# Two fused transformer blocks on one core: the modulation, the state-space quarters and the key selection are put in another order on five engines

## The chip, the cores and the metric

The kernel runs on one core of a Trainium2 chip. The time is device microseconds for one execution. The core has TensorE (matmuls and transposes, named PE in the profile; its weight loads are PEld), VectorE (DVE), ScalarE (ACT), GpSimd (POOL) and SyncE (SP), which here only issues DMAs. Each engine runs its own list of instructions in order; semaphores tie the lists together. All arithmetic is float32.

## The reference

Two blocks in series on x of 512 rows by 1024. Only block one is touched by the change.

```
mod = silu(c) @ w_ada + b_ada                  # shift, scale, gate: 3 x 1024
h = rms_norm(x, norm_g) * (1 + scale) + shift
u, z, q, k, v, az, q_idx, k_idx, w_idx = split(h @ w_in)   # 512 each; k_idx 64, w_idx 8
y = s5(u) + d_skip * u                         # 32 groups of 16 channels, 64 complex states
y = gelu(y); y_ssm = y * sigmoid(y @ w_glu + b_glu) * silu(z)
score = sum over heads of w_idx * relu(q_idx . k_idx), causal; sel = top 128 keys of each query
y_attn = softmax(q . k / 8 + rel_bias, over sel) @ v * silu(az)   # 8 heads of 64, q and k normed
x = x + gate * (concat(y_ssm, y_attn) @ w_out)
x = second_block(x)                            # sparse attention, pooling mixer, conv feed-forward
```

## The kernel before

Everything lives in one SBUF arena; two slots of 2 MB take turns for the weights (chunks `u`, `qi`, `ki`, `k`, `v`, `q`, `az`, `z`, `gate0`, `gate1`, `glu`, `out0`, `out1`, ...), loaded by SyncE, a chunk two places on waiting for the last matmul on the one that it replaces. PSUM banks 0 to 3 take the projections (`name_proj`), banks 4 to 7 the transposes and the small products (`name_aux`); TensorE must take the names in the order in which they were given. `proj_ready`/`aux_ready` wait for TensorE to have filled a bank, `proj_out`/`aux_out` for it to have been emptied. `step` puts a semaphore wait between two instructions of one engine that depend on each other. The order within each engine is written out by hand.

**Start.** x arrives as four row tiles. ScalarE squares and sums each (L1233). VectorE turns the sums into means (`x_mean`), GpSimd raises them to -0.5 (L1593), and VectorE (tiles 0 and 2, L1869) and ScalarE (tiles 1 and 3, L1236) scale x. TensorE turns x (eight banks, `x_turns`), ScalarE copies it out to hT. The modulation is w_ada times silu(c), in four parts of 2 MB: VectorE's `mod_sums(s)` is eight 128x512 multiply-adds (L1851, L1854) into `macc[s % 2]`, TensorE's `mod_turn(s)` adds over the partitions (L773), VectorE's `mod_cols(s)` and `h_odd` and ScalarE's `h_even` apply the result to hT. Parts 0 and 1 serve the first half of the channels, so that `u_step(0)` can begin; parts 2 and 3 serve `u_step(1)`. Between the two u steps TensorE turns the state-space matrices b and c (L732, L788) and the relative bias (L794). VectorE then makes the tables of powers; its `prep_done` lets GpSimd begin.

**The state-space product** goes by quarters q of eight groups. GpSimd makes `CL` (three 128x1152 operations, L1624 to L1626) and `Zt` (three 128x1024, L1634 to L1636), then `r8` and `E1`, `E2` (seven of about 512, L1641 to L1652). TensorE's `ssm_kernels(q)` makes the taps from CL and turns Zt; `ssm_chunks(q)` gives the chunk inputs; GpSimd rotates them (L1660 to L1663), VectorE scans (`scan(q)`, L1994), GpSimd rotates back (L1665 to L1668, `s_done`), with two swaps of halves through DMAs of SyncE (`ssm_swap`). `ssm_out(q)` on TensorE needs `s_done` and the spread taps (`ssm_spread`), and reads CL as well; `ssm_back(q)` takes y out over DRAM to where VectorE's `gelu_in(q)` reads it. There is one CL, so that GpSimd begins quarter q + 1 when TensorE has finished `ssm_out(q)`.

**Attention of block one.** `rels(i, ...)` are the index heads of query block i (1 to 3; eight heads), taken by ScalarE with relu into two buffers `reluq` and summed by VectorE (`scores(i)`, L2001 to L2010). `topk(i, rounds)` takes eight keys a round (maximum, L2016; replacement, L2017) over 256, 384 or 512 columns, 16 rounds each. `head_norm` squares, sums, takes the root of (eleven small steps, L1774 to L1779) and scales (L2033) q or k; TensorE turns k (`kt`) and q (`qt`) after it. Then 16 pairs of heads are worked off: scores, two filler matmuls (L967, L969: the gate and the GLU), turned weights, values. The first filler waits for `silb_done`, which VectorE gives after its work on the mixer. The rounds of block 3 lie in part between the first three pairs, and `gelu_in(3)`, `gelu_out(3)` at pairs 1 and 3. After the pairs comes the output projection, and from there on block two.

## Time and profile before

| | us |
|---|---|
| median of three runs | 1527.62 |
| the three runs | 1523.86, 1527.62, 2513.14 |
| the profiled execution | 1530.01 |
| its span, first to last instruction | 1528.2 |
| TensorE busy in it | 1441.4 (94%) |
| VectorE, ScalarE, GpSimd busy | 631.3, 317.1, 262.8 |
| mean granted clock of TensorE | 0.970 |

The profiled execution is one run; the times of single instructions below come from it. A busy TensorE counts waiting out a slow clock as busy: a matmul takes twice as long at 1.2 GHz (granted clock 0.50) as at 2.4 GHz (1.00).

### The profile page before, as it was taken

How to read it: one execution, taken by the hardware profiler on the slowest of the kernel's cores; microseconds unless marked ns; L12 is line 12 of the kernel's file. 1: busy time of each engine (PE TensorE's matmuls, PEld its weight loads, DVE VectorE, ACT ScalarE, POOL GpSimd, SP SyncE). 2: the span in 40 equal slices, each digit the busy share in tenths (PEclk: the TensorE clock that was granted, in tenths of full speed). 3: DMA queues.
4: the chain of work that ended last, by engine and by line, in shares of the span. 5: the costliest groups of instructions: out<-in, count | busy, mean ns of one | idle time of the engine just before them, and what ended most of it. 6: DMA issues, size and time to landing. Idle time of an engine off the chain costs nothing.

```text
span 1528.2 us, 13916 instructions
## 1 busy us (share of the span) xinstructions
PE 1441.4 (94%) x5076; PEld 723.4 (47%) x5076; DVE 631.3 (41%) x1533; ACT 317.1 (21%) x773; POOL 262.8 (17%) x257
## 2 busy tenths in 40 slices
PE   2799999969999998998999999998999999989999
PEld 2444455534545446454555565444444444434343
DVE  6571759888431660033456673112323333230000
ACT  3111232114200002202456662001111111110000
POOL 1053627624102478000000000000000000000000
PEclk9799999979999998999999999999999999999999
DMA  9345233442312222102110001203113132121220
GB/s 325 119 104 157 69 84 96 137 132 76 138 33 68 77 89 74 64 1 83 56 50 7 1 2 56 101 9 110 55 57 108 55 102 63 42 110 38 89 87 27
DMA packets 85630, 120.43 MB, mean 79 GB/s; under 512 B 15128, under 2 KB 43102, under 8 KB 85564
## 3 DMA queue, kind: packets, MB, share of 16 engines
q1 hardware_dynamic: 79088, 109.89, 22.4%
q10 hardware_dynamic: 4732, 5.97, 1.2%
q0 software_dynamic: 1744, 3.70, 0.8%
q8 instruction: 41, 0.67, 0.2%
q14 instruction: 25, 0.20, 0.0%
HBM read 111.00 MB, written 6.84 MB: 77 GB/s over the span
## 4 chain that ended last, share of the span: by engine, by line
PE 86%; DVE 8%; ACT 2%; issue 2%; DMA 1%; POOL 0%; SPq 0%; ACTq 0%; DVEq 0%
PE bank L1198 20%; PE bank L704 19%; PE bank L1208 10%; PE bank L714 6%; PE bank L1157 5%; PE bank L732 4%; PE bank L999 4%; PE bank L1113 3%; PE bank L1137 3%; PE bank L763 2%; PE bank L1011 2%; PE bank L872 1%; DVE arena L1854 1%; PE bank L1095 1%; DVE arena L2017 1%
## 5 line engine op out<-in xcount | busy, mean ns | idle before, releaser
L704 PE MATMUL bank<-arena 128*128 128x512 f32 (+1 forms) x752 | 319.0, 584 | 3.4 <-ACT arena L1459 3.0
L1198 PE MATMUL bank<-arena 128*128 128x512 f32 (+1 forms) x704 | 302.5, 592 | 1.5 <-ACT arena L1453 1.5
L704 PEld LDWEIGHTS bank<-arena 128*128 128x128 f32 x752 | 143.0, 192 | 167.6 <-issue 162.5
L1198 PEld LDWEIGHTS bank<-arena 128*128 128x128 f32 (+1 forms) x704 | 131.9, 188 | 171.5 <-issue 171.5
L1208 PE MATMUL bank<-arena 128*128 128x512 f32 (+1 forms) x352 | 156.0, 602 | 5.0 <-DVE arena L2401 4.0
L732 PE MATMUL bank<-arena 128*128 128x128 f32 (+2 forms) x692 | 98.5, 283 | 35.3 <-ACT arena L1236 10.6
L732 PEld LDWEIGHTS bank<-arena 128*128 128x128 f32 (+2 forms) x692 | 84.1, 146 | 91.0 <-issue 43.1
L2390 DVE SCALAR_TENSOR_TENSOR arena<-bank,arena 128x511 f32<-128x511 f32 (+1 forms) x44 | 33.0, 749 | 211.9 <-ACT arena L1572 211.9
L714 PE MATMUL bank<-arena 128*128 128x512 f32 x256 | 111.5, 593 | 0.0
L1208 PEld LDWEIGHTS bank<-arena 128*128 128x128 f32 (+1 forms) x352 | 66.1, 191 | 95.0 <-issue 90.1
L1593 POOL TENSOR_TENSOR arena<-arena 128x1 f32<-128x1 f32 x12 | 8.1, 682 | 509.9 <-DVE arena L1785 496.6
L2373 DVE SCALAR_TENSOR_TENSOR arena<-bank,arena 128x512 f32<-128x512 f32 x16 | 11.1, 692 | 203.0 <-PE bank L1208 152.3
L1572 ACT ACTIVATE arena<-bank,arena 128x512 f32<-128x512 f32 (+1 forms) x44 | 34.2, 777 | 258.6 <-PE bank L1198 258.6
L1534 ACT ACTIVATE arena<-arena 128x128 f32<-128x128 f32 (+3 forms) x128 | 70.9, 555 | 73.2 <-DVE arena L2321 73.2
L1157 PE MATMUL bank<-arena 128*128 128x512 f32 x160 | 85.2, 639 | 0.6 <-DVE arena L2356 0.5
L2321 DVE CUSTOM_DVE_ANT_0 arena<-bank,arena 128x128 f32<-128x128 f32 (+3 forms) x128 | 57.8, 489 | 62.3 <-PE bank L1113 61.5
L714 PEld LDWEIGHTS bank<-arena 128*128 128x128 f32 x256 | 48.1, 190 | 57.9 <-issue 57.9
L999 PE MATMUL bank<-arena 128*128 128x512 f32 x128 | 55.7, 593 | 0.5 <-issue 0.5
L1113 PE MATMUL bank<-arena 64*128 64x128 f32 (+3 forms) x256 | 51.8, 481 | 1.2 <-ACT arena L1524 1.2
L1546 ACT ACTIVATE arena<-bank 128x128 f32<-128x128 f32 (+3 forms) x128 | 47.9, 424 | 19.3 <-PE bank L732 19.3
L1137 PE MATMUL bank<-arena 128*64 128x128 f32 x640 | 48.9, 282 | 0.0
L2335 DVE TENSOR_SCALAR arena<-arena 128x128 f32<-128x128 f32 (+3 forms) x128 | 43.7, 384 | 2.3
(307 smaller groups left out, 1497.7 us busy)
## 6 DMA issues: line engine op xcount, KB each, us to landing
arena<-in_w_in SPq DMA_DIRECT2D x14, 2048.0 KB, 7.8
arena<-in_w_up SPq DMA_DIRECT2D x20, 1024.0 KB, 6.8
arena<-in_w_ada SPq DMA_DIRECT2D x8, 1024.0 KB, 14.4
arena<-in_w_down SPq DMA_DIRECT2D x4, 2048.0 KB, 7.7
arena<-in_w_ada SPq DMA_DIRECT2D x2, 2048.0 KB, 8.3
arena<-in_w_out SPq DMA_DIRECT2D x2, 2048.0 KB, 7.9
arena<-in_w_attn_br SPq DMA_DIRECT2D x2, 2048.0 KB, 8.8
arena<-in_w_o SPq DMA_DIRECT2D x2, 2048.0 KB, 7.7
```

Of the source, the lines that this page charges most:

```text
L704: mm = pe.matmul(ps[:, 0:n], act[:, k, 128 * t:128 * t + 128], w[:, k, 0:n], start=(k == 0), stop=(k == kt - 1))
L714: mm = pe.matmul(ps[:, :], w[:, k, 128 * j:128 * j + 128], act[:, k, :], start=(k == 0), stop=(k == kt - 1))
L732: mm = pe.transpose(ps[0:f, at:at + p], b, ident[0:p, 0:p] if eye is None else eye)
L999: mm = pe.matmul(ps[:, :], a[:, 128 * t:128 * t + 128], w[:, k, :], start=(n == 0), stop=(n == KT - 1))
L1113: pe.matmul(bank[2 * (n % 2) + e][:, 0:128 * (i + 1)], qT2[r, p, 128 * i:128 * i + 128], ksT[r, 2 * b + p // 4, 0:128 * (i + 1)], start=Tr ...
L1137: mm = pe.matmul(ps[64 * e:64 * e + 64, 0:128], vs2[:, b, m, 64 * g:64 * g + 64], pT2[:, n % 2, e, 128 * m:128 * m + 128], start=False, st ...
L1157: mm = pe.matmul(fbank(key)[:, :], act_[:, k, 128 * t:128 * t + 128], w[:, k, :], start=(k == 0), stop=(k == kt - 1))
L1198: mm = pe.matmul(ps[0:m, :], w[:, k, c0:c0 + m], hT[:, k, :], start=(k == 0), stop=(k == KT - 1))
L1208: mm = pe.matmul(banks[t][:, :], aT[0:m, k, 128 * t:128 * t + 128], w[0:m, k - 8 * b, :], start=(k == 0), stop=(k == FT - 1))
L1534: act.activation(buf, buf, ACT.Exp, scale=-1.0, bias=sml[:, c0:c0 + 1], accum_out=sml[:, c1:c1 + 1]).then_inc(exp2_done, 1)
L1546: act.activation(pT2[:, n % 2, e, 0:128 * (i + 1)], abank(("pt2", n, e))[:, 0:128 * (i + 1)], ACT.Copy).then_inc(afree(("pt2", n, e)), 1)
L2321: v.tensor_tensor_reduce(pr2[:, n % 3, e, 0:cols], bank[2 * (n % 2) + e][:, 0:cols], trim[:, 512 - cols:512], -1.0, 3.0e38, ALU.add, ALU.m ...
```

## The change

It does four things, all in block one.

1. At the start GpSimd makes mean and root of each row tile itself and ScalarE scales all four; VectorE does neither. The loads of b and c go from ScalarE's queue to SyncE's, ahead of the load of u's weights and of modulation parts 2 and 3. TensorE turns c, b and the relative bias before `mod_turn(0)`, and VectorE's `mod_cols(2)` comes after the cosine instead of ahead of `mod_sums(3)`.
2. CL gets a second buffer (in qiT, so that quarter 1 waits for the last index head). GpSimd begins quarter q when it has finished the rotations of quarter q - 1 and `ssm_out(q - 2)` is done.
3. The index heads run beside k's projection instead of v's, and `scores` and the selection come earlier on VectorE: all of block 3's rounds lie ahead of `scan(2)`, q's norm and the pairs. The quarters are spread anew over the projections on TensorE, ScalarE and SyncE; the bias load (2 MB, `biasT`) is issued earlier and waits for `r8_done`.
4. `gelu_in` has three operations instead of four, the constant going into tanh's scale, and all four channels' GELU lie ahead of the pairs.

The diff, cut to its core; the bank names (`name_aux`) follow the new order, and `CLs[q % 2]` stands for CL in `ssm_taps` and `ssm_out`:

```diff
@@ -119,6 +119,7 @@
 Wn = z.take(1024, QG, 128)
+CLs = [CL, qiT.rearrange("p a b -> p (a b)")[:, 0:QG * 9 * GC].rearrange("p (a b c) -> p a b c", a=QG, b=9)]
 KX0 = z.at
@@ -576,6 +578,12 @@
     ada_load(1)
+    for a, src in enumerate((b_re, b_im)):
+        for half in range(2):
+            sp_.dma_start(braw[a][0:32, 1024 * half:1024 * half + 1024],
+                          src[0].rearrange("g p i -> g (p i)")).then_inc(b_in, 16)
+    for a, src in enumerate((c_re, c_im, c_re)):
+        sp_.dma_start(craw[:, :, a, :], src[0].rearrange("(m g) o p -> (g o) m p", g=8)).then_inc(craw_in, 16)
     wu_load(0)
@@ -631,18 +639,18 @@
             ssm_swap(0)
+            ssm_back(0)
         if name == "az":
-            ssm_back(0)
             ssm_spread(1)
+            ssm_swap(1)
         if name == "z":
-            ssm_swap(1)
             ssm_back(1)
-        if name == ("gate", 0):
             ssm_spread(2)
             ssm_swap(2)
+        if name == ("gate", 0):
             ssm_back(2)
+            ssm_spread(3)
         if name == ("gate", 1):
-            ssm_spread(3)
             ssm_swap(3)
@@ -793,6 +797,10 @@
                   start=True, stop=True).then_inc(aux_done, 1)
+    pe.wait_ge(pool_ones, 1)
+    mod_turn(0)
+    mod_turn(1)
+    u_step(0)
     mod_turn(2)
@@ -856,18 +864,11 @@
     ssm_kernels(0)
-    one_rows("k", 0, "k", hT)
-    ssm_chunks(0)
-    one_rows("k", 1, "k", hT)
-    one_rows("k", 2, "k", hT)
-    one_rows("k", 3, "k", hT)
-    ssm_out(0)
-    one_rows("v", 0, "v", hT)
...
-        w = weights(pe, "v")
-        ps = begin_proj(("v", t)) if half == 0 else pbank(("v", t))
+        w = weights(pe, "k")
+        ps = begin_proj(("k", t)) if half == 0 else pbank(("k", t))
         for k in range(4 * half, 4 * half + 4):
@@ -886,39 +887,45 @@
     for i in range(1, TT):
-        half_rows(i, 0)
+        half_rows(i - 1, 0)
         rels(i, range(0, 4))
-        if i == 2:
-            ssm_kernels(1)
-        half_rows(i, 1)
+        half_rows(i - 1, 1)
         rels(i, range(4, 8))
+        if i == 1:
+            ssm_chunks(0)
+    ssm_out(0)
+    one_rows("k", 3, "k", hT)
+    one_rows("v", 0, "v", hT)
+    ssm_kernels(1)
+    one_rows("v", 1, "v", hT)
     ssm_chunks(1)
+    one_rows("v", 2, "v", hT)
+    one_rows("v", 3, "v", hT)
     pe.wait_ge(knorm_done, TT)
...
         turn(("kt", m), [row[:, t, 128 * m:128 * m + 128] for t in range(TT)])
+    ssm_out(1)
     one_rows("q", 0, "q", hT)
     one_rows("q", 1, "q", hT)
-    ssm_out(1)
+    ssm_kernels(2)
     one_rows("q", 2, "q", hT)
+    ssm_chunks(2)
     one_rows("q", 3, "q", hT)
-    ssm_kernels(2)
     one_cols("az", 0, "az", hT)
-    ssm_chunks(2)
     one_cols("az", 1, "az", hT)
+    ssm_out(2)
     pe.wait_ge(qnorm_done, TT)
...
     one_cols("az", 2, "az", hT)
-    ssm_out(2)
+    ssm_kernels(3)
     one_cols("az", 3, "az", hT)
+    ssm_chunks(3)
     one_cols("z", 0, "z", hT)
-    ssm_kernels(3)
     one_cols("z", 1, "z", hT)
-    ssm_chunks(3)
+    ssm_out(3)
     one_cols("z", 2, "z", hT)
     one_cols("z", 3, "z", hT)
-    ssm_out(3)
-
     def pair_scores(n):
@@ -1231,15 +1238,9 @@
         act.activation(sqx, xrow[:, t, :], ACT.Square, accum_out=stat[:, t:t + 1]).then_inc(sq_done, 1)
-    for t in (1, 3):
+    for t in range(TT):
         act.wait_ge(root_done, t + 1)
         act.activation(xrow[:, t, :], xrow[:, t, :], ACT.Copy, scale=stat[:, t:t + 1]).then_inc(xn_done, 1)
-    for a, src in enumerate((b_re, b_im)):
-        for half in range(2):
-            act.dma_start(braw[a][0:32, 1024 * half:1024 * half + 1024],
-                          src[0].rearrange("g p i -> g (p i)")).then_inc(b_in, 16)
-    for a, src in enumerate((c_re, c_im, c_re)):
-        act.dma_start(craw[:, :, a, :], src[0].rearrange("(m g) o p -> (g o) m p", g=8)).then_inc(craw_in, 16)
@@ -1263,19 +1262,19 @@
            .then_inc(afree(f"bt{a}"), 1)
+    for name, c0, n in (("rb", 0, 512), ("rb2", 512, 128)):
+        aux_ready(act, name)
+        act.activation(rb_row[0:8, c0:c0 + n], abank(name)[0:8, 0:n], ACT.Copy).then_inc(afree(name), 1)
+    h_even(0)
+    h_even(2)
     for at, n, src in ROWS2:
...
             act.dma_start(colr[at:at + 1, 64 * half:64 * half + 64], src).then_inc(rows2_in, 16)
-    for name, c0, n in (("rb", 0, 512), ("rb2", 512, 128)):
-        aux_ready(act, name)
-        act.activation(rb_row[0:8, c0:c0 + n], abank(name)[0:8, 0:n], ACT.Copy).then_inc(afree(name), 1)
     aux_out(act, "rb")
...
     act.dma_start(rb_one_dram, rb_row[0:8, :]).then_inc(rb_saved, 16)
-
-
     h_even(4)
@@ -1363,52 +1362,54 @@
+    def gelu_tanh(j):
+        act.wait_ge(y_skip, j + 1)
+        act.activation(gt[:, j % 2, :], gt[:, j % 2, :], ACT.Tanh, scale=SQ2PI * 0.044715).then_inc(y_tanh, 1)
+
     ssm_kernels(0)
-    rows_in_("k", row, (0,))
-    ssm_chunks(0)
-    rows_in_("k", row, (1, 2, 3))
-    ssm_out(0)
-    rows_in_("v", v1, (0,))
     for i in range(1, TT):
         rels(i, range(0, 4))
-        if i == 2:
-            ssm_kernels(1)
-        rows_in_("v", v1, (i,))
+        rows_in_("k", row, (i - 1,))
         rels(i, range(4, 8))
+        if i == 1:
+            ssm_chunks(0)
+    ssm_out(0)
+    rows_in_("k", row, (3,))
+    rows_in_("v", v1, (0,))
+    ssm_kernels(1)
+    rows_in_("v", v1, (1,))
     ssm_chunks(1)
+    rows_in_("v", v1, (2, 3))
     act.wait_ge(gbias_done, 1)
...
     aux_ready(act, ("kt", 3))
+    ssm_out(1)
     rows_in_("q", row, (0, 1))
-    ssm_out(1)
-    rows_in_("q", row, (2, 3))
     ssm_kernels(2)
+    rows_in_("q", row, (2,))
+    ssm_chunks(2)
+    rows_in_("q", row, (3,))
+    gelu_tanh(0)
+    gelu_tanh(1)
     az_in(0)
-    ssm_chunks(2)
     az_in(1)
+    ssm_out(2)
     columns_in("qt", qT, colv[:, CV_GQ:CV_GQ + 1])
     az_in(2)
-    ssm_out(2)
+    ssm_kernels(3)
+    act.wait_ge(r8_done, NQ)
+    act.wait_ge(rb_spread, 16)
+    act.dma_start(biasT, bass.AP(rb_dram.tensor, 127, [[639, 128], [81920, 8], [1, 512]])).then_inc(bias_in, 16)
     az_in(3)
+    ssm_chunks(3)
+    gelu_tanh(2)
     z_in(0)
-    ssm_kernels(3)
     z_in(1)
-    def gelu_tanh(j):
...
-    ssm_chunks(3)
-    gelu_tanh(0)
-    gelu_tanh(1)
+    ssm_out(3)
     act.wait_ge(e_done, NQ)
-    act.wait_ge(rb_spread, 16)
-    aux_out(act, ("z", 3, 1))
-    act.dma_start(biasT, bass.AP(rb_dram.tensor, 127, [[639, 128], [81920, 8], [1, 512]])).then_inc(bias_in, 16)
     z_in(2)
-    gelu_tanh(2)
     z_in(3)
-    ssm_out(3)
+    gelu_tanh(3)
@@ -1596,7 +1595,11 @@
-    x_roots()
+    for t in range(TT):
+        pool.wait_ge(sq_done, t + 1)
+        step(pool.tensor_scalar(stat[:, t:t + 1], stat[:, t:t + 1], 1.0 / D, EPS, ALU.mult, ALU.add))
+        pool.tensor_tensor(stat[:, t:t + 1], stat[:, t:t + 1], halves[:, 0:1], ALU.pow).then_inc(root_done, 1)
+
     def consts_load():
@@ -1618,12 +1621,16 @@
             pool.memset(r8[:, :, 0:1], 0.0).then_inc(pool_ones, 1)
+        elif q == 1:
+            aux_ready(pool, ("rel", 3, 7))
         else:
-            aux_ready(pool, ("y", q - 1))
+            aux_ready(pool, ("y", q - 2))
+        if q:
+            pool.wait_ge(s_done, q)
...
         step(pool.tensor_tensor(g2v, Xa[1], Pa[1], ALU.mult))
-        step(pool.tensor_tensor(CL, g1v, g2v, ALU.add))
+        step(pool.tensor_tensor(CLs[q % 2], g1v, g2v, ALU.add))
         pool.sem_inc(cl_done, 1)
@@ -1631,6 +1638,8 @@
         g2v = g2[:, 0:1024].rearrange("p (a b c) -> p a b c", a=QG, b=L)
+        if q:
+            aux_ready(pool, ("z", q - 1, 1))
         pool.tensor_tensor(g1v, Ya[0], Pa[0], ALU.mult)
@@ -1765,7 +1775,7 @@
-    roots = [0]
+    roots = [TT]
@@ -1859,14 +1864,7 @@
     mul(t_(TH), t_(LI), t_(DT))
-    x_mean(0)
-    x_mean(1)
     exp_(t_(ER), t_(XR))
-    x_mean(2)
-    x_mean(3)
-    for t in (0, 2):
-        v.wait_ge(root_done, t + 1)
-        v.tensor_scalar(xrow[:, t, :], xrow[:, t, :], stat[:, t:t + 1], None, ALU.mult).then_inc(xn_done, 1)
     mod_sums(0)
@@ -1885,7 +1883,6 @@
     step(v.scalar_tensor_tensor(t_(SIN), p, 1.0, r, ALU.add, ALU.mult))
-    mod_cols(2)
     mod_sums(3)
@@ -1915,6 +1912,7 @@
+    mod_cols(2)
     mod_cols(3)
@@ -2049,8 +2047,8 @@
         step(v.tensor_tensor(gt[:, j % 2, :], y, y, ALU.mult))
-        step(v.tensor_scalar(gt[:, j % 2, :], gt[:, j % 2, :], 0.044715, 1.0, ALU.mult, ALU.add))
-        v.tensor_tensor(gt[:, j % 2, :], gt[:, j % 2, :], y, ALU.mult).then_inc(y_skip, 1)
+        v.scalar_tensor_tensor(gt[:, j % 2, :], gt[:, j % 2, :], 1.0 / 0.044715, y, ALU.add, ALU.mult)\
+            .then_inc(y_skip, 1)
@@ -2064,38 +2062,36 @@
-    scan(0)
-    head_norm("k", None, knorm_done, row)
     v.wait_ge(consts_in2, 80)
...
     scores(2, 8)
+    scan(0)
     scores(3, 16)
+    topk(1, TOPK // 8, True)
+    head_norm("k", None, knorm_done, row)
+    topk(2, 6)
     scan(1)
-    topk(1, TOPK // 8, True)
-    topk(2, 8)
+    topk(2, TOPK // 8 - 6, True)
+    topk(3, TOPK // 8, True)
+    gelu_in(0)
+    gelu_in(1)
+    scan(2)
     head_norm("q", None, qnorm_done, row)
-    scan(2)
     az_in(0)
     az_in(1)
-    topk(2, TOPK // 8 - 8, True)
-    az_in(2)
-    gelu_in(0)
-    topk(3, 3)
-    az_in(3)
-    gelu_in(1)
-    topk(3, 4)
-    z_in(0)
-    z_in(1)
-    scan(3)
     aux_ready(v, ("qt", 3))
...
     gelu_in(2)
-    z_in(2)
-    z_in(3)
-    topk(3, 6)
+    az_in(2)
+    az_in(3)
+    scan(3)
     gelu_out(2)
+    for j in range(4):
+        z_in(j)
+    gelu_in(3)
+    gelu_out(3)
@@ -2150,20 +2146,13 @@
     v.wait_ge(bias_in, 16)
-    left = TOPK // 8 - 13
     for n in range(NS1 + 4):
...
             pair_logits(n)
-        if n < left:
-            topk(3, 1, n == left - 1)
-        if n == 1:
-            gelu_in(3)
         if 0 <= n - 1 < NS1:
             pair_normed(n - 1)
-        if n == 3:
-            gelu_out(3)
         if n < NS1:
```

## Rows read from the trace of the kernel before

**Rows 1.** Windows by stage: busy time (instructions) per engine, granted clock, DMA share, GB/s.
```profile
0.00:21.40 21.40, 1.00 (x4) 0.64 (x4) 9.17 (x42) 8.47 (x13) 5.37 (x14) 1.00 0.91 309
21.40:87.20 65.80, 50.27 (x174) 29.89 (x174) 45.42 (x123) 13.30 (x24) 5.03 (x4) 0.79 0.52 181
...
124.00:328.50 204.50, 192.70 (x693) 103.35 (x692) 147.02 (x239) 42.94 (x80) 106.83 (x65) 0.95 0.35 96
328.50:401.00 72.50, 66.23 (x364) 34.43 (x364) 57.77 (x153) 33.45 (x101) 24.35 (x24) 0.96 0.33 115
401.00:1528.20 1127.20, 1096.31 (x3759) 540.38 (x3759) 353.13 (x913) 214.96 (x549) 98.17 (x130) 0.98 0.18 61
```

**Rows 2.** Waits of TensorE, whole span: releaser, total us, times, longest.
```profile
PE bank L773 <- DVE arena L1854: 11.4, 2, 6.6
PE bank L732 <- ACT arena L1236: 10.6, 1, 10.6
```

**Rows 3.** Timeline of the start: start us, us, engine, line, operation, count, idle before.
```profile
11.82 1.06 ACT L1233 ACTIVATE arena<-arena 128x1024 f32<-128x1024 f32 x1
...
20.20 1.15 ACT L1236 ACTIVATE arena<-arena 128x1024 f32<-128x1024 f32 x1 [2.91 <-POOL arena L1593]
20.56 5.54 DVE L1854 SCALAR_TENSOR_TENSOR arena<-arena 128x512 f32<-128x512 f32 x7
...
35.65 16.84 PE L763 MATMUL bank<-arena 128*128 128x512 f32 x32 [1.64 <-ACT arena L1247]
...
52.32 1.04 PE L732 MATMUL bank<-arena 128*128 128x128 f32 x8
...
58.10 1.54 PE L773 MATMUL bank<-arena 128*128 128x1 f32 x8
...
66.25 1.87 PE L773 MATMUL bank<-arena 128*128 128x1 f32 x8 [6.61 <-DVE arena L1854]
...
70.59 16.43 PE L763 MATMUL bank<-arena 128*128 128x512 f32 x32 [2.47 <-ACT arena L1247]
...
87.13 27.73 PE L714 MATMUL bank<-arena 128*128 128x512 f32 x64
```

**Rows 4.** Timeline of GpSimd, its second quarter of the state-space work.
```profile
159.75 2.25 POOL L1624 TENSOR_TENSOR arena<-arena 128x1152 f32<-128x1152 f32 x1 [10.87 <-PE bank L844]
...
183.45 1.44 POOL L1652 TENSOR_TENSOR arena<-arena 128x512 f32<-128x512 f32 x1
...
222.29 1.27 POOL L1668 TENSOR_TENSOR arena<-arena 128x512 f32<-128x512 f32 x1
```

**Rows 5.** Timeline of VectorE during the same stretch of GpSimd.
```profile
159.89 2.15 DVE L1779 SCALAR_TENSOR_TENSOR arena<-arena 128x32 f32<-128x32 f32 x1
...
164.28 0.19 DVE L1778 SCALAR_TENSOR_TENSOR arena<-arena 128x32 f32<-128x32 f32 x1
...
167.03 8.30 DVE L2033 TENSOR_TENSOR arena<-arena 128x512 f32<-128x512 f32 x4
```

**Rows 6.** Timeline of VectorE: scan, selection of blocks 1 and 2, q's norm, GELU.
```profile
216.81 1.23 DVE L1994 TENSOR_TENSOR_SCAN arena<-arena 128x512 f32<-128x512 f32 x1 [6.27 <-POOL arena L1663]
...
234.72 0.55 DVE L2016 MAX8 arena<-arena 128x8 f32<-128x384 f32 x1
...
244.72 0.71 DVE L2026 TENSOR_TENSOR arena<-arena 128x512 f32<-128x512 f32 x1
...
259.81 1.21 DVE L1994 TENSOR_TENSOR_SCAN arena<-arena 128x512 f32<-128x512 f32 x1
...
272.98 2.19 DVE L2050 SCALAR_TENSOR_TENSOR arena<-arena 128x512 f32<-128x512 f32 x1
```

**Rows 7.** Timeline of TensorE: filler matmuls of the first, sixth and seventh attention pairs.
```profile
328.53 3.47 PE L967 MATMUL bank<-arena 128*128 128x512 f32 x4 [4.39 <-DVE arena L2116]
...
349.08 1.98 PE L967 MATMUL bank<-arena 128*128 128x512 f32 x4
...
352.22 1.98 PE L967 MATMUL bank<-arena 128*128 128x512 f32 x4
```

More of the change, by code:

```diff
@@ L226, in rel_names @@
             return [("rel", i, h) for h in range(8)]
-        name_aux("ccol", "lam", "cols", *[("x", k) for k in range(KT)], ("mod", 0), ("mod", 1),
-                 "c1", "c2", "bt0", "bt1", "rb", "rb2", ("mod", 2), ("mod", 3), "cols2")
+        name_aux("ccol", "lam", "cols", *[("x", k) for k in range(KT)], "c1", "c2", "bt0", "bt1",
+                 "rb", "rb2", ("mod", 0), ("mod", 1), ("mod", 2), ("mod", 3), "cols2")
         name_proj(*four("u"), *four("qi"), "ki", *four("k"), *four("v"), *four("q"), *four("az"), *four("z"))
-        name_aux("wi", *ssm_names(0), ("v", 0), ("y", 0), *rel_names(1), *rel_names(2)[:4], *ssm_names(1),
-                 *rel_names(2)[4:], *rel_names(3), ("v", 1), *four("kt"), ("y", 1), *ssm_names(2), ("v", 2),
-                 *four("qt"), ("y", 2), *ssm_names(3), ("v", 3), ("y", 3))
+        name_aux("wi", *ssm_names(0), *rel_names(1), ("v", 0), *rel_names(2), *rel_names(3), ("y", 0), *ssm_names(1),
+                 ("v", 1), *four("kt"), ("y", 1), *ssm_names(2), ("v", 2), ("y", 2), *four("qt"), *ssm_names(3),
+                 ("v", 3), ("y", 3))
         SUB1 = [(i, p) for i in range(TT) for p in range(4)]
@@ L432, in program @@
         e_done = sem("e_done")
+        r8_done = sem("r8_done")
         consts_in = sem("consts_in")
@@ L775, in mod_turn @@
                 mm.then_inc(aux_done, 1)
-            pe.wait_ge(pool_ones, 1)
-            mod_turn(0)
-            mod_turn(1)
-            u_step(0)
             pe.wait_ge(craw_in, 48)
@@ L1435, in _ @@
                     pair_exp(n)
-                if n == 2:
-                    gelu_tanh(3)
                 if n >= 2:
@@ L1640, in _ @@
                     pool.wait_ge(tables_done, 1)
-                pool.tensor_copy(r8[:, :, 1:NCH], sp[:, 12, gs].unsqueeze(2).broadcast_to((128, QG, NCH - 1)))
+                pool.tensor_copy(r8[:, :, 1:NCH], sp[:, 12, gs].unsqueeze(2).broadcast_to((128, QG, NCH - 1)))\
+                    .then_inc(r8_done, 1)
                 shape = (128, QG, 8, 8)
```

12 lines of the change are left out of this document (2 added, 10 removed).

## The prediction

> **What bounds the kernel now.** I read the windows by stage first [rows 1]. From 401 us to the end TensorE is busy 1096 of 1127 us: the change touches nothing there, so every gain or loss is made before 401, and it reaches the end only as far as it moves the moment at which the output projection starts. Between 21.4 and 401 TensorE idles 15.5 us at the start, 11.8 in the middle, 6.3 in the pairs, and its granted clock averages 0.79, 0.95 and 0.96: slow matmuls count as busy. The reader should see that the middle, 124.0 to 328.5, needs 192.7 busy less 0.05 x 204.5 lost to the slow clock, so 182.5 us of TensorE at 2.4 GHz: the floor for any order of the same work. The waits [rows 2] name what to shorten: two for the last modulation multiply-add (11.4 us), one for ScalarE's scaling of x (10.6); a third stands ahead of the first filler, for `silb` (4.39) [rows 7]. The timelines [rows 3 to 7] give the prices.
>
> **Start.** TensorE gets x at 21.35, when the fourth scaling ends (1.15 us each) [rows 3]. The last square is over at about 12.9 (11.82 and 1.06) [rows 3]; GpSimd's two tiny operations per tile are not shown as a pair, and lie between 0.3 and 2 us. Even at 2 they stay ahead of ScalarE, so four scalings in a row end at 17.6, or at 20 at the worst. VectorE loses four one-column operations and two scalings, about 2.5 us with their waits, so `mod_sums(0)` starts at 17.7 and two of them (6 us each: 5.54 and the first multiply) end at 29.8 instead of 32.1, if the 6 MB of x and parts 0 and 1 are there: at the 309 GB/s of the first window [rows 1] they take 19.4 us and land near 23, while the second part is needed at 23.8. The 0.9 MB of b and c now stand ahead of u's weights and part 2 in SyncE's queue and add some 3 us to these; seven issues of half a microsecond are the same again. Part 2 is wanted only at 33.5, so I cost this at nothing; without that cover it is 3 us.
>
> The turns of c, b and bias (52.32 to 58.10, so 5.8 us) now fill TensorE while it waits for part 1. `u_step(0)` can start at 33.5 (35.65 before), and since TensorE worked until then, at full clock: half of the 27.73 us for 64 is 13.9, where it took 16.84 [rows 3]. It ends at 47.4, and `mod_turn(2)` follows at once, not at 58.10. VectorE's `mod_sums(2)`, sine (2.4) and `mod_sums(3)` run 33.5 to 48.1 without waiting for it; from the end of the last one to the next u step it took 4.3 us (66.25 to 70.59). So `u_step(1)` starts near 52.5 and ends between 66.4 and 69; I take 67.5, against 87.1. **Gain 19.6 us**, bounds 15 and 22. The quarters' first kernel, at 124.0 before, is then due at 104.
>
> **Middle, if only TensorE counted.** A projection group costs 6.93 (27.73 / 4) [rows 3]; twenty make 138.6. The other 44 us I split into 9 for the 24 index heads, 8 for each quarter (2.9 kernels, 1.7 chunks, 3.4 out) and 2 for each turn. Without waits z's last group would end at 104 + 182.5 = 286.5. I don't believe that, because the new order makes one long list on VectorE, and it has to be walked through.
>
> **The list on VectorE.** First the prices. Selection of block 1 costs 16.7 (218.0 to 234.72), a round over 384 columns 1.25 (10.0 / 8), one over 512 then 1.5, 24.3 for 16 with the same step on. q's norm took 15.1 (244.72 to 259.81) with GpSimd half busy beside it [rows 6]. From a scan's start to `s_done` it is 6.75 (216.81 to 223.56) [rows 4, 6]. And GpSimd matters: while its 13 operations of a quarter ran (25.1 us, 159.75 to 184.9) [rows 4], steps of 0.19 us took 2.15 and 2.49, four scalings 8.30; one of 0.19 slipped through where GpSimd waited on its own result [rows 5]. The selection is not touched: block 2's rounds in rows 6 ran beside GpSimd's third quarter and took the 1.25 us that they took elsewhere.
>
> Here the second CL does harm. GpSimd now starts quarter q right after the rotation of q - 1: quarter 1 when the last head is done, quarter 3 some 7 us after `scan(2)`.
> - Last head on TensorE: 104 + 2.9 + 3 x 6.93 + 9 + 1.7 = 138.4. Quarter 1 starts there and hits the last four operations of `scores(3)`, at 2.5 us each: done at 148.5 (142 if they slip ahead).
> - Block 1 16.5, k's norm 13 (GpSimd ends at 163.5), six rounds 7.5: `scan(1)` at 185.3, `s_done` at 192.
> - TensorE wants `ssm_out(1)` at 138.4 + 3.4 + 5 x 6.93 + 2.9 + 1.7 + 2 = 183. It idles 9 us, and comes back at the slow clock: 2.8 (16.84 and 16.43 against 13.9) [rows 3].
> - VectorE: scan, ten rounds, 16 rounds, two `gelu_in` (one operation less each, 4.5 with some blocking): `scan(2)` at 231.5. GpSimd's quarter 3 starts at 238.5. The squares of q's norm take 5.8 and are over just then; the eleven root steps and four scalings are all behind GpSimd. One per GpSimd operation with a slip at its five own waits puts the fifteenth at the tenth or eleventh operation, about 22 us on: q's norm done at **261**.
> - TensorE wants q's turn at 192 + 6.2 + 6 x 6.93 + 4.6 + 3.4 = 248. It idles 13 us, slow again for 2.8.
> - Then 2 + 6 x 6.93 + 2.9 + 1.7 + 3.4 + 2.8: z's last group ends at 315.5. Quarter 3 is not late: `scan(3)` waits for `ssm_chunks(3)`, two groups ahead of `ssm_out(3)`, and the bias load of 2 MB is mostly past.
> - The tail hangs on VectorE: copy-out, `z_in(3)`, three for `gelu_in(3)`, tanh, `gelu_out(3)`, `silb`, eight of 0.7 (as 0.71) [rows 6]: first filler at 321, against 328.5.
>
> In the waits that are added, ScalarE stands at `gelu_tanh(0)` and at `r8_done` with az, `ssm_out` and the bias load behind it; both come before the banks are wanted. SyncE's new order holds az's weights behind `scan(1)` and z's behind `scan(2)`; both are wanted over 25 us later, and a load of 2 MB at the first window's rate takes 7 [rows 1]. I cost them at nothing.
>
> **Pairs.** The first five took 4.1 us each (328.53 to 349.08) with selection rounds and GELU between, the sixth 3.1 [rows 7]; without these, five at 3.1: **gain 5 us**, between 2 and 6.
>
> Sum: 328.5 - 321 = 7.5, and 5: 12.5 us. Against the profiled 1530.0 (span 1528.2) that is 1517.5; against the median 1527.6, 1515.
>
> The Trainium skill, "SBUF — State Buffer", section "Who interferes with whom", says that a VectorE instruction with two SBUF inputs, or in a two-port mode, is blocked for the whole of a GpSimd instruction that reads SBUF, and holds GpSimd off in turn. By that, without slips, fifteen steps would take 15 x 1.93 = 29 us, an estimate, and the time would be near 1522; the 0.19 at 164.28 speaks for slips, so I keep 22, and this case stays inside the forecast's own range.
>
> **Rivals.**
> A. *TensorE-bound after all.* The norm and scores escape GpSimd (its operations may leave gaps, or `scan(2)` is later than its squares). Then 286.5 + 5.5 = 292, 36.5 gained, and 5: 1486. For it: the index heads now come ahead of k's norm and beside k's projection, so VectorE starts its list well before TensorE needs any of it. Against: rows 5. It needs over 20 us less on the list.
> B. *The start gives less.* The clock falls between the u steps, c comes late, part 3 arrives late: 104 becomes 112, and the list moves along unshortened: 1523.
> C. *Slower: q's norm is the bound.* With 512-wide operations against the large ones a step took 2.19 us and more (the first of `gelu_in(0)`) [rows 6]. At 2.5 for each of the fifteen it is 37.5 instead of 22, and the tail of quarter 3 then meets GELU and `az_in` as well (4 us): 1534. It decides when q's norm ends after 273, 12 us later than I have it.
> D. *The early GELU and selection change nothing* (something else holds the first filler at 328): only the pairs' 5 us: 1523, with B.
>
> **Chances.** Forecast 0.53 (1503 to 1526), A 0.20, B and D 0.14, C 0.13. To hold 8 in 10 I take in half of A and most of C: 1488 to 1533. Faster by over 2% (below 1497) needs A or its neighbourhood, 0.25; slower by over 2% (above 1558) nothing here reaches, 0.03; within 2%, which is about what a measurement here can tell from no change, 0.72.
>
> **What would show it.** In the changed profile: x turned from about 17.6; `u_step(1)` ending near 67; the first kernel near 104; TensorE idle ahead of `ssm_out(1)` and of q's turn, released by GpSimd's last operation of the back-rotation and by the scaling in `head_norm`; root steps of 1.5 to 2.5 us there; first filler near 321; five pairs in 15.5 us. Wrong if the two idle stretches are missing (then A), or if the start keeps its idle time.

## The result and the profile after

The changed kernel takes 1546.9 us (median of 4 runs, 1545.6 to 1548.1) against 1527.4 for the kernel before (median of 4 runs): a ratio of 1.0135, with a 95% interval of 1.0115 to 1.0156. It is 1.35% slower, where 1515 was forecast. One run of the kernel before took 2513 us; it was disturbed, and the ratio leaves it out.

The profiled execution took 1548.1 us, with a span of 1546.3, so 18.1 more than before. I read the windows by stage first, as in [rows 1]:

```profile
17.40:75.00 57.60, 49.28 (x173) 29.71 (x173) 44.08 (x123) 13.70 (x24) 2.43 (x3) 0.82 0.71 233
75.00:111.90 36.90, 35.02 (x86) 14.72 (x87) 21.50 (x68) 4.16 (x7) 25.61 (x22) 1.00 0.62 137
111.90:350.90 239.00, 199.26 (x693) 108.92 (x692) 144.52 (x250) 44.24 (x81) 104.39 (x65) 0.89 0.34 93
350.90:419.10 68.20, 65.23 (x364) 34.44 (x364) 51.33 (x138) 33.16 (x100) 24.33 (x24) 0.96 0.25 87
419.10:1546.30 1127.20, 1096.50 (x3759) 540.21 (x3759) 353.18 (x913) 214.96 (x549) 98.05 (x130) 0.98 0.18 61
```

The last stage is 1127.2 us in both kernels, so the whole loss stands before the output projection, which starts at 419.1 and not at 401.1. The stage in the middle has the same 693 matmuls as before [rows 1], but 239.0 us instead of 204.5: TensorE idles 39.7 us there instead of 11.8, and its granted clock is 0.89 instead of 0.95.

| us | before | forecast | after |
|---|---|---|---|
| start of the quarters' first kernel | 124.0 | 104 | 111.9 |
| from there to the first filler | 204.6 | 217 | 239.1 |
| from there to the output projection | 72.5 | 67.5 | 68.2 |
| sum | 401.1 | 388.5 | 419.1 |

The waits of TensorE from 75 to 351 us name the middle's four idle stretches (line, releaser; total, times, longest); the last row is the wait ahead of the first filler, at the end of the middle:

```profile
PE bank L850 <- issue: 16.2, 2, 9.7
PE bank L740 <- DVE arena L2031: 12.7, 1, 12.7
PE bank L873 <- DMA arena<-arena: 5.7, 1, 5.7
PE bank L974 <- DVE arena L2112: 3.6, 1, 3.6
```

L850 is `ssm_out`, which waits twice (9.7 and 6.6 us), L740 a turn (here q's), L873 a half group of k ahead of the index heads, L974 the filler. "Issue" means that the profile names no releaser; GpSimd's last operation of the back-rotation ends 0.1 us before each of the two `ssm_out` starts. TensorE's timeline shows where they stand and what the clock adds behind each:

```profile
17.40 6.01 PE L740 MATMUL bank<-arena 128*128 128x128 f32 x32 [8.46 <-ACT arena L1243]
28.61 1.97 PE L740 MATMUL bank<-arena 128*128 128x128 f32 x8 [5.19 <-DMA arena<-in_c_re]
...
36.41 3.57 PE L781 MATMUL bank<-arena 128*128 128x1 f32 x16
41.54 16.21 PE L771 MATMUL bank<-arena 128*128 128x512 f32 x32 [1.56 <-ACT arena L1248]
...
60.98 13.97 PE L771 MATMUL bank<-arena 128*128 128x512 f32 x32 [1.56 <-ACT arena L1248]
...
111.88 1.92 PE L819 MATMUL bank<-arena 128*16 128x128 f32 x16
...
120.48 5.69 PE L873 MATMUL bank<-arena 128*128 128x512 f32 x8 [5.66 <-DMA arena<-arena]
...
127.17 3.70 PE L873 MATMUL bank<-arena 128*128 128x512 f32 x8
...
209.41 0.66 PE L850 MATMUL bank<-arena 128*128 128x64 f32 x2 [9.67 <-issue]
...
216.26 15.88 PE L712 MATMUL bank<-arena 128*128 128x512 f32 x32
...
280.53 3.67 PE L740 MATMUL bank<-arena 128*128 128x128 f32 x16 [12.74 <-DVE arena L2031]
283.99 7.53 PE L722 MATMUL bank<-arena 128*128 128x512 f32 x16
...
323.35 0.66 PE L850 MATMUL bank<-arena 128*128 128x64 f32 x2 [6.57 <-issue]
...
330.20 15.23 PE L722 MATMUL bank<-arena 128*128 128x512 f32 x32
...
350.95 3.78 PE L974 MATMUL bank<-arena 128*128 128x512 f32 x4 [3.61 <-DVE arena L2112]
```

Two of the stretches were forecast (ahead of `ssm_out(1)` and of q's turn), two were not. Ahead of the heads TensorE waits for `ki_twice`, ScalarE's copy of ki into the upper partitions. Before the change k's four groups and the first of v stood between ki and the heads and hid it, though the copy took 6.5 us there too. Ahead of `ssm_out(3)` the cause is one engine back. GpSimd's rotation of quarter 3 waits 8.9 us for SyncE's swap:

```profile
303.71 1.27 POOL L1670 TENSOR_TENSOR arena<-arena 128x512 f32<-128x512 f32 x1 [20.88 <-ACT arena L1309]
313.89 1.26 POOL L1672 TENSOR_TENSOR arena<-arena 128x512 f32<-128x512 f32 x1 [8.91 <-DMA arena<-arena]
```

The queue of SyncE shows why (start, length of the issue, line, count). L679 is the first 2 MB of gate's weights, L607 the first of quarter 3's two swaps, issued behind it, L611 the second:

```profile
301.30 0.40 SPq L679 DMA_DIRECT2D arena<-in_w_ada  x1
303.65 1.14 SPq L607 DMA_DIRECT2D arena<-arena  x2
317.78 1.10 SPq L611 DMA_DIRECT2D arena<-arena  x2
```

Q's norm on VectorE, the forecast's largest term, went as written. Of the eleven root steps, 0.19 us each when nothing holds them, four took 0.19 us, one 0.5 and the other six 1.4 to 2.5; the four scalings took 7.5 us, where four beside an idle GpSimd take 2.5:

```profile
259.18 1.39 DVE L1784 TENSOR_SCALAR arena<-arena 128x32 f32<-128x32 f32 x1
260.60 2.17 DVE L1785 TENSOR_SCALAR arena<-arena 128x32 int32<-128x32 int32 x1
262.81 0.19 DVE L1787 TENSOR_TENSOR arena<-arena 128x32 f32<-128x32 f32 x1
263.03 2.50 DVE L1788 SCALAR_TENSOR_TENSOR arena<-arena 128x32 f32<-128x32 f32 x1
...
272.98 7.49 DVE L2031 TENSOR_TENSOR arena<-arena 128x512 f32<-128x512 f32 x4
```

From 259.18 to 280.39 the fifteen steps took 21.2 us.

### The profile page after: what moved, and what is told of

It reads as the page before. It is cut to its first block, busy times and chain, and to the rows that moved or that the text cites. A ratio compares the mean times of both kernels' runs of the same rounds, so it can differ in the third digit from the quotient of the medians.

```text
span 1546.3 us, 13908 instructions
## 1 busy us (share of the span) xinstructions
PE 1446.3 (94%) x5076; PEld 728.6 (47%) x5076; DVE 620.8 (40%) x1523; ACT 320.5 (21%) x775; POOL 260.2 (17%) x261
## 4 chain that ended last, share of the span: by engine, by line
PE 89%; DVE 4%; issue 2%; ACT 2%; DMA 2%; SPq 1%; POOL 0%; DVEq 0%; ACTq 0%
PE bank L712 20%; PE bank L1205 20%; PE bank L1215 10%; PE bank L722 6%; PE bank L1164 5%; PE bank L740 4%; PE bank L1006 4%; PE bank L1120 3%; PE bank L1144 3%; PE bank L771 2%; PE bank L1018 2%; PE bank L873 2%; PE bank L974 1%; PE bank L1102 1%; PE bank L1048 1%
## 5 line engine op out<-in xcount | busy, mean ns | idle before, releaser
L740 PE MATMUL bank<-arena 128*128 128x128 f32 (+2 forms) x692 | 101.7, 289 | 47.2 <-DVE arena L2031 12.7
L740 PEld LDWEIGHTS bank<-arena 128*128 128x128 f32 (+2 forms) x692 | 87.2, 150 | 101.1 <-issue 43.0
L2362 DVE SCALAR_TENSOR_TENSOR arena<-bank,arena 128x512 f32<-128x512 f32 x16 | 11.1, 692 | 203.0 <-PE bank L1215 152.3
## 6 DMA issues: line engine op xcount, KB each, us to landing
arena<-in_w_ada SPq DMA_DIRECT2D x8, 1024.0 KB, 12.8
```

Of the source, the lines that this page charges most:

```text
L740: mm = pe.transpose(ps[0:f, at:at + p], b, ident[0:p, 0:p] if eye is None else eye)
```

## The experiments

All changes are made to the changed kernel unless the text says otherwise. Each kernel was timed beside the kernel before on the same chip. "Against before" is the ratio with its 95% interval; "loss" is the difference of the two medians (19.5 us for the changed kernel). The intervals reach 2 to 4 us to either side, for four_mended and best_order 5 to 6.

**Theory 1**: TensorE waits for VectorE's list, and GpSimd's early quarters stretch it. **Theory 2**: the list is too long in its new order. **Third**: transfers that have lost their cover or their place.

### gpsimd_waits

```diff
-    elif q == 1:
-        aux_ready(pool, ("rel", 3, 7))
     else:
-        aux_ready(pool, ("y", q - 2))
-    if q:
-        pool.wait_ge(s_done, q)
+        aux_ready(pool, ("y", q - 1))
```

> Only change against the changed kernel: GpSimd starts quarter q when the product of quarter q - 1 is complete, as before, and no longer right after the back-rotation (the two CL buffers stay). Theory 1 (the early quarters of GpSimd stretch VectorE's list of small steps, and TensorE waits for that list): the last four operations of scores(3) take some 3 us instead of 9.1, the idle stretch ahead of ssm_out(1) falls from 9.7 to 2 or less, that ahead of q's turn from 12.7 to 3 or less, each with some 2 to 3 us of slow clock; 18 to 26 us faster than the changed kernel, near 1525. Theory 2 (the list is simply too long in its new order, GpSimd or not): both stretches stay over 7 us, and the time is within 5 us of 1547. Against both: if GpSimd's quarters now come too late for the kernels' turns, TensorE waits at L819 and the time rises.

1533.6 us; 1.0038 (1.0023 to 1.0054) against before: 12.8 us of the loss go, less than the 18 to 26 expected. VectorE's last four operations of `scores(3)` are short, as expected:

```profile
154.52 3.32 DVE L1998 SCALAR_TENSOR_TENSOR arena<-arena 128x512 f32<-128x512 f32 x4 [1.61 <-ACT arena L1362]
```

Q's turn has no wait left. But TensorE still stands 6.2 us at `ssm_out(1)`, where 2 or less had been expected, and there is a new wait for GpSimd's products, which now come too late for quarter 3's inputs:

```profile
205.40 0.66 PE L850 MATMUL bank<-arena 128*128 128x64 f32 x2 [6.17 <-issue]
...
279.19 1.97 PE L740 MATMUL bank<-arena 128*128 128x128 f32 x8 [5.00 <-POOLq L1642]
```

The stretch ahead of `ssm_out(3)` fell too, from 6.6 to 3.1 us, so that not all of the 12.8 us is VectorE's list. But q's turn is free of its wait, so theory 1 holds, and the second CL has a use: it only starts quarters 1 and 3 at a bad moment. The next two take them apart.

### quarter3_later and quarter1_later

```diff
 # quarter3_later
+    if q == 3:
+        pool.wait_ge(qnorm_done, TT)
     if q:
         pool.wait_ge(s_done, q)
 # quarter1_later
     elif q == 1:
-        aux_ready(pool, ("rel", 3, 7))
+        aux_ready(pool, ("y", 0))
```

> Only change: GpSimd starts quarter 3 when q's norm is done, no longer right after the back-rotation of quarter 2. The norm should take 13 us instead of 29, the idle stretch ahead of q's turn (12.7 us) and its slow clock go, and a wait of 1 to 3 us for GpSimd's sixth operation stands ahead of the inputs of quarter 3. If this collision is the largest single price of the change: 10 to 13 us faster. If q's norm is late for the length of VectorE's list: under 4 us.

1531.9 us; 1.0022 (1.0011 to 1.0034) against before: 16 us of the loss go, more than expected. The scalings take 2.5 us, and TensorE turns q without a wait; the wait for the products is 0.5 us. The stretch ahead of `ssm_out(3)` is still 6.3 us, so none of this gain comes from there:

```profile
262.28 2.50 DVE L2033 TENSOR_TENSOR arena<-arena 128x512 f32<-128x512 f32 x4
```

```profile
268.36 1.92 PE L740 MATMUL bank<-arena 128*128 128x128 f32 x16
...
279.45 1.09 PE L740 MATMUL bank<-arena 128*128 128x128 f32 x8 [0.46 <-POOLq L1648]
```

> Only change against the changed kernel: GpSimd starts quarter 1 when the product of quarter 0 is complete (3.5 us later), no longer when the last index head is. The last four operations of scores(3) should take 3.3 us instead of 9.1, but k's norm then meets the end of quarter 1, so that the idle stretch ahead of ssm_out(1) falls only from 9.7 to about 6: 3 to 5 us faster. If contention on scores(3) passes through whole: 8 us faster.

1542.8 us; 1.0086 (1.0068 to 1.0105) against before: 5.3 us of the loss go, just above what was expected. The last four operations of `scores(3)` took 3.3 us instead of 9.1, and the stretch ahead of `ssm_out(1)` fell to 6.2, as expected. But k's norm met the end of quarter 1: its four scalings took 4.6 us, where the changed kernel has 2.5.

```profile
183.35 4.64 DVE L2031 TENSOR_TENSOR arena<-arena 128x512 f32<-128x512 f32 x4
```

### scan_first

```diff
-    topk(2, 6)
     scan(1)
+    topk(2, 6)
```

> Only change against the changed kernel: on VectorE scan(1) stands ahead of the first six selection rounds of block 2, not behind them. scan(1) should start at about 195 instead of 202.5 us, so the idle stretch ahead of ssm_out(1) falls from 9.7 to about 2 and its slow clock goes too. Theory 1 (VectorE's list as a whole is the bound up to q's norm): the list's end ahead of scan(2) doesn't move (246.6), so scan(2) comes only 4 us earlier, the idle stretch ahead of q's turn grows from 12.7 to some 18, and the gain is 3 to 5 us. Rival (each wait costs what it shows): 10 us faster.

1541.8 us; 1.008 (1.0055 to 1.0104) against before: 7.6 us of the loss go when each kernel is set against its own runs of the kernel before, 5.1 when the medians of the two kernels are compared directly. Both lie above the 3 to 5 of theory 1 and under the rival's 10. The trace decides more clearly than the time:

```profile
200.46 0.41 PE L850 MATMUL bank<-arena 128*128 128x64 f32 x2 [2.15 <-issue]
...
273.71 3.67 PE L740 MATMUL bank<-arena 128*128 128x128 f32 x16 [18.76 <-DVE arena L2031]
```

The stretch ahead of `ssm_out(1)` fell from 9.7 to 2.2 us, as expected, and the one ahead of q's turn grew from 12.7 to 18.8 (expected 18). A wait on TensorE is not its own price while one list feeds the next wait as well.

### k_ahead and copy_ahead

Two ways to take away the same wait for `ki_twice`:

```diff
 # k_ahead, TensorE (ScalarE's copies in the same order)
+    half_rows(0, 0)
+    half_rows(0, 1)
     pe.wait_ge(ki_twice, 16)
     for i in range(1, TT):
-        half_rows(i - 1, 0)
+        half_rows(i, 0)
...
-    one_rows("k", 3, "k", hT)
 # copy_ahead, SyncE, ahead of its load of v's weights
+    if name == "v":
+        sp_.wait_ge(ki_twice, 16)
```

> Only change: k's first row group is projected whole ahead of TensorE's wait for the copy of ki, the other three between the heads. It hides the 5.7 us wait and the slow half group behind it (2.2 us), but the heads end no earlier (about 154.2 against 155.2 us), so VectorE's list starts at the same time. Theory 1 (VectorE's list sets the time of ssm_out(1)): gain 0 to 2 us; the idle stretch ahead of ssm_out(1) grows from 9.7 to about 16. Rival (each wait of TensorE costs what it shows): 7 to 8 us faster.

1547.3 us; 1.0129 (1.01 to 1.0158) against before: no change. The 5.7 us are gone from the trace and nothing is gained. That VectorE's list sets the time is borne out; where the time went is only partly what I had expected, since the stretch ahead of `ssm_out(1)` is 10.5 us and not 16, and there is a new wait of 2.8 us for GpSimd ahead of quarter 1's inputs.

```profile
168.31 1.97 PE L740 MATMUL bank<-arena 128*128 128x128 f32 x8 [2.83 <-POOLq L1647]
...
205.63 0.66 PE L850 MATMUL bank<-arena 128*128 128x64 f32 x2 [10.53 <-issue]
```

> Only change: the queue of SyncE loads v's weights (2 MB) after the copy of ki has landed, not ahead of it. The copy should land 2 to 4 us after its issue instead of 9.8, TensorE's idle 5.7 us ahead of the heads and the slow half group go, and the heads and with them VectorE's list come 7 to 8 us earlier. Theory 1 (the list sets the time): 7 to 8 us faster. Rival (the copy is late for another reason than the load of v's weights): no change, wait still over 4 us.

1541.0 us; 1.009 (1.0064 to 1.0115) against before: 5.3 us of the loss go, a little under the 7 to 8. TensorE's wait is gone. From the quarters' first kernel to the end of the last head it is 35.4 us in this trace, against 43.4 in the changed kernel and 42.3 in k_ahead: here VectorE's list really starts earlier, in k_ahead it hardly does. The rows of DMA issues give the size of the copy and the time from its issue to its landing, in the changed kernel and in this one:

```profile
arena<-arena ACTq DMA_DIRECT2D x1, 128.0 KB, 9.8
```

```profile
arena<-arena ACTq DMA_DIRECT2D x1, 128.0 KB, 2.8
```

The copy was slow because 2 MB for v, which nobody needs for another 50 us, had been issued 0.6 us ahead of it. That it stands in another engine's queue didn't help. The Trainium skill says so, "DMA: Bandwidth & Descriptors", section "Issuing engines are not separate DMA queues": transfers started by any engine end on the same 16 DMA engines. The two traces agree, with 9.8 against 2.8 us. How long the copy takes beside v's weights varies, though: 5.8 to 8.8 us in the other traces in which v's weights go first.

### swap_ahead

```diff
     if name == ("gate", 0):
         ssm_back(2)
         ssm_spread(3)
+        ssm_swap(3)
     if name == ("gate", 1):
-        ssm_swap(3)
         ssm_back(3)
```

> Only change: in SyncE's queue the two swaps of quarter 3 stand ahead of the load of gate's first weights (2 MB). If the collision with 2 MB loads makes the swap late: the swap lands within 4 us instead of 10, the 6.6 us idle ahead of ssm_out(3) go or fall below 2, and z's last two groups run at full clock: 6 to 10 us faster. If the bias load (2 MB, issued 9 us ahead of the swap on another queue) is what holds it: the wait stays over 4 us and the gain is under 3. If VectorE's tail after ssm_out(3) is the bound anyway: wait gone, gain under 3.

1538.4 us; 1.0065 (1.0046 to 1.0085) against before: 7.9 us of the loss go, as expected. GpSimd waits 1.7 us for the swap instead of 8.9, and TensorE has no wait at `ssm_out(3)`:

```profile
305.89 1.26 POOL L1672 TENSOR_TENSOR arena<-arena 128x512 f32<-128x512 f32 x1 [1.73 <-DMA arena<-arena]
```

The bias load, also 2 MB and issued at 294.5 us in the changed kernel, stood where it was in this run: by itself it wasn't the cause. Whether gate's weights alone would make the swap late, without the bias load under way, wasn't tried.

### start_alone and c_ahead

start_alone is the kernel before with the start of the change only. In c_ahead SyncE's queue is `ada_load(0)`, then b and c, then `ada_load(1)`:

```diff
 ada_load(0)
-ada_load(1)
 for a, src in enumerate((b_re, b_im)): ...
 for a, src in enumerate((c_re, c_im, c_re)): ...
+ada_load(1)
 wu_load(0)
```

> The kernel before with the start of the change alone: x scaled by ScalarE with GpSimd making mean and root, b and c loaded through SyncE's queue, turns of c, b and bias ahead of the first turned modulation piece, third piece's copy-out later. Everything from the quarters' first kernel on stands as before. Theory 1 (the start keeps the 12 us that the changed kernel's trace shows, first quarter's kernel at 112 instead of 124, and the loss is made later): 9 to 13 us faster than the kernel before, near 1516. Rival (the start's gain is given back by the weights and projections that follow, whatever their order): within 3 us of the kernel before.

1519.4 us; 0.9931 (0.9905 to 0.9957) against before: 10.6 us faster. This part of the change is a gain by itself, so all the rest together costs 30 us.

> Only change against the changed kernel: b and c are loaded ahead of the second modulation part, not behind it. c's turns begin at 23.5 instead of 28.6 us and u_step(0) at 35 instead of 41.5; the quarters' first kernel comes near 106 instead of 112, and since nothing behind it is tied to absolute time, 5 to 7 us faster. Rival (the second part comes later and VectorE's multiply-adds with it): under 2 us.

1542.9 us; 1.0087 (1.007 to 1.0104) against before: 5.2 us of the loss go, the lower end of what was expected. c's turns begin at 23.6 and `u_step(0)` at 35.6, as expected; TensorE idled only 1.2 us ahead of c. Yet `u_step(0)` (L771) is as slow as in the changed kernel, and the quarters' first kernel comes at 109.2, not near 106:

```profile
23.58 1.09 PE L740 MATMUL bank<-arena 128*128 128x128 f32 x8 [1.16 <-DMA arena<-in_c_re]
...
35.62 16.45 PE L771 MATMUL bank<-arena 128*128 128x512 f32 x32 [1.56 <-ACT arena L1248]
```

### four_mended, best_order, rounds_in_pairs

four_mended puts gpsimd_waits, copy_ahead, swap_ahead and c_ahead together. best_order goes on from it:

```diff
+    elif q == 1:
+        aux_ready(pool, ("y", 0))
     else:
-        aux_ready(pool, ("y", q - 1))
+        aux_ready(pool, ("y", q - 2))
+    if q == 3:
+        pool.wait_ge(qnorm_done, TT)
+    if q:
+        pool.wait_ge(s_done, q)
 # VectorE
-    topk(2, 6)
     scan(1)
+    topk(2, 6)
...
-    topk(3, TOPK // 8, True)
+    topk(3, 6)
...
     az_in(2)
+    topk(3, 5)
     az_in(3)
+    topk(3, TOPK // 8 - 11, True)
     scan(3)
...
-    for j in range(4):
+    for j in range(3):
         z_in(j)
     gelu_in(3)
+    v.wait_ge(aux_done, AUX[("y", 3)] + 1)
+    v.tensor_copy(silb, silc[:, 0:8].unsqueeze(2).broadcast_to((128, KT, 128))).then_inc(silb_done, 1)
+    z_in(3)
     gelu_out(3)
-    v.wait_ge(aux_done, AUX[("y", 3)] + 1)
-    v.tensor_copy(silb, silc[:, 0:8].unsqueeze(2).broadcast_to((128, KT, 128))).then_inc(silb_done, 1)
```

(GpSimd's quarter 2 starts early again, quarters 1 and 3 don't.) rounds_in_pairs is best_order with block 3's last five rounds in the first five pairs, one each.

> The changed kernel with GpSimd's later quarters, v's weights behind the copy of ki, quarter 3's swaps ahead of gate's weights, and in the start c and b loaded ahead of the second modulation part. If the effects add, 13 (measured) + 6 (measured) + 6 to 9 (measured 8.6 alone, but 3.5 of its wait had gone with GpSimd's later quarters) + 3 to 5 for the start: 1547 less 28 to 33, so 1514 to 1519. For the start alone: c's turns begin near 23.5 instead of 28.6 us, u_step(0) near 36.5 instead of 41.5, at full clock, and the quarters' first kernel near 107. If instead the early small-row loads of b and c hold up the second modulation part, u_step(0) stays at 41 and the sum is 1520 or more.

1513.6 us; 0.9898 (0.9862 to 0.9933) against before: 16.4 us faster than before. That is 35.9 us below the changed kernel, where the four edits one by one gave 31.2; the difference is inside the intervals.

> The mended kernel, further: quarter 3 of GpSimd waits for q's norm rather than for the product, quarter 2 starts early as in the changed kernel, scan(1) ahead of the six rounds, ten of block 3's sixteen rounds moved into VectorE's idle time after q's norm, and the copy of silb and gelu_in(3) ahead of z's last group on VectorE. If VectorE's list was the only bound left in the middle, TensorE's idle stretches there fall to under 4 us together, the wait ahead of the first filler from 3.6 to under 1.5, and the time is 12 to 18 us below the mended kernel: 1498 to 1506. If the moved rounds hold up az_in or scan(3), a new wait stands ahead of ssm_out(3), and the gain is under 8.

1496.4 us; 0.9783 (0.9742 to 0.9824) against before: 33.6 us faster, and 17 below four_mended, as expected. The quarters' first kernel now comes at 104.6, and of TensorE's idle stretches over 0.5 us from there to the pairs one is left ahead of `ssm_out(3)` (3.3), and one of 1.4 ahead of the first pair. The first two rows are from the start; the last two are the fillers of the first and the sixth pair:

```profile
17.12 6.72 PE L742 MATMUL bank<-arena 128*128 128x128 f32 x40 [6.65 <-ACT arena L1245]
...
34.30 16.11 PE L773 MATMUL bank<-arena 128*128 128x512 f32 x32 [1.56 <-ACT arena L1250]
...
275.10 0.66 PE L852 MATMUL bank<-arena 128*128 128x64 f32 x2 [3.29 <-issue]
...
298.94 1.98 PE L976 MATMUL bank<-arena 128*128 128x512 f32 x4
...
312.43 1.99 PE L976 MATMUL bank<-arena 128*128 128x512 f32 x4
```

> The best order with block 3's last five selection rounds back in the first five attention pairs, one in each, everything else the same. If a round in a pair costs TensorE what the profile of the kernel before suggested (1.5 us of VectorE, of which the pairs of 3.1 us hide part): 2 to 5 us slower than the best order, pairs of 3.5 to 4.1 us. If VectorE has room in the pairs: no change, and the gain of the change's pairs came from GELU alone.

1489.4 us; 0.9738 (0.9723 to 0.9752) against before. I had expected it slower than best_order by 2 to 5 us; it is faster by 3.6 us in the spans of the two profiles (1487.9 and 1491.5) and by 6.9 in the medians. The two intervals overlap, so that a gain over best_order is not shown by the times alone; that it is not 2 to 5 us slower is. In its trace the first five pairs take 15.7 us against 13.5, so the rounds do cost 2.2 us there:

```profile
293.95 3.27 PE L976 MATMUL bank<-arena 128*128 128x512 f32 x4
...
309.64 1.98 PE L976 MATMUL bank<-arena 128*128 128x512 f32 x4
```

But those five rounds had stood ahead of `scan(3)`, where they held up `ssm_out(3)`: its wait went from 3.3 to 0.3 us, and the slow clock behind it with it, so that the time from the quarters' first kernel to the first filler fell by 7.4 us. My expectation counted only the place that the rounds came to, and not the place that they left. rounds_in_pairs has the lowest median of all the versions, 39 us under the kernel before.

## Why the prediction was wrong

The forecast said 12.5 us of gain, and the trace has 18.1 of loss: 30.6 us are missing. By its own steps, the price of a stretch being its idle time and what TensorE's slow clock adds behind it:

| step | forecast | measured | missing |
|---|---|---|---|
| Start | -20 | -12.1 | 7.9 |
| copy of ki ahead of the heads | 0 | 5.7 + 2.0 | 7.7 |
| `ssm_out(1)` | 9 + 2.8 | 9.7 + 5.1 | 3.0 |
| q's turn | 13 + 2.8 | 12.7 + 2.3 | -0.8 |
| `ssm_out(3)` | 0 | 6.6 + 4.5 | 11.1 |
| Pairs | -5 | -4.3 | 0.7 |

These are 29.6 of the 30.6 us. (The slow clock: the half group 5.69 against the 3.70 of the next, `ssm_out` 6.85 against the 3.62 of `ssm_out(0)`, pairs of groups 15.88 and 15.23 against 13.95, the turn 3.67 against 1.91.)

**Start: two steps failed.** The first is "I cost this at nothing; without that cover it is 3 us". x was turned from 17.40, as forecast at 17.6. But the cost of b and c was looked for at the wrong place, in what stands behind them. They themselves were late: their seven issues took 9.1 us of SyncE's queue and not 3.5, c came at 28.6, and its turns, which now stand ahead of the first modulation turn, held that until 36.4, though `mod_sums(1)` was over at 29.4. c_ahead shows what the place in the queue was worth (5.2), start_alone that the rest of the gain is real (10.6).

The second is "since TensorE worked until then, at full clock". `u_step(0)` took 16.2 us and not 13.9. TensorE's 5.2 us of idle time ahead of c aren't the reason: with 1.2 us in c_ahead it took 16.45, and in best_order, where TensorE idled no more than 0.3 us from 17.12 to 32.7, still 16.1. In best_order the granted clock was 1.00 while x, c and b were turned (to 27.4 us), 0.59 from there to 33.0, with the bias and the 128x1 modulation turns, and 0.50 over the first 4 us of `u_step(0)`. It took 15.4 us or more in every trace of this case. So filling TensorE with these small matmuls didn't bring the full clock; why the clock fell among them is open.

**The list on VectorE: right.** Both idle stretches stand at the places that were forecast, with 9.7 and 12.7 us for 9 and 13, and the fifteen steps of q's norm took 21.2 us, against 22 forecast. Everything came later than forecast, the last head at 155.2 instead of 138.4 and q's norm at 280.5 instead of 261, but TensorE and VectorE were late together, and the stretches between them held. The prediction's estimate from the Trainium skill ("SBUF — State Buffer", section "Who interferes with whom"), taken without slips, gave 29; the row of 0.19 us decided, and rightly. quarter3_later and quarter1_later show that it is GpSimd's early start that stretches the list. It is also the largest price that a single edit gave back: quarter 3 started later returns 16 of the 19.5 us.

**"Quarter 3 is not late": this step failed, and is the largest of the missing terms.** It counted two groups between `ssm_chunks(3)` and `ssm_out(3)` and looked at one transfer, the bias load. It didn't walk SyncE's queue in the new order past quarter 3, where gate's 2 MB come ahead of the swap. The paragraph on added waits names that queue for az and z, and stops there. swap_ahead settles it: the wait is gone, and 7.9 us with it.

**The copy of ki was not in the forecast at all.** k's projection was moved from between ki and the heads to between the heads, and with it went the cover of a transfer that no wait of the trace before showed. copy_ahead and k_ahead show that its price is not the idle time itself but the later start of VectorE's list: both take the wait away, and only the one that brings the heads forward gains.

**Pairs** were right in place and size (16.2 us for the five intervals, 15.5 forecast). Rival C was not what happened: q's norm ended at 280.5, after the 273 from which it should decide, but because everything ahead of it was late, not because it was slow. The range (1488 to 1533) failed because it held no case in which waits came up that no row of before shows. The prediction's split of the middle adds up to 45 us and not 44; that changes nothing here.

The table reads one trace, and its first two rows vary. In the eight traces with the same start as the changed kernel the quarters' first kernel comes between 110.7 and 115.6 us. In the seven traces with the same order around the copy of ki, the wait ahead of the heads and the slow clock behind it are 7.7 us in the changed kernel, between 0 and 7.3 in the others, and 4.7 in the mean. That fits the 5.3 us that copy_ahead gave back. Of the start's 7.9 us, 2.3 are the slow `u_step(0)`, which c_ahead left as it was; the rest fits its 5.2. The slow clock behind `ssm_out(1)`, 5.1 us where 2.8 were taken from the start's rows, is 4.4 to 5.6 us in the seven other traces that wait there for 6 us or more; it wasn't tried by itself. Open is why the clock stays slow in `u_step(0)`.
